# Two transformer blocks on one core: gate tiles in the scan's last quarter, attention turns further behind their scaling, inverse roots by logarithm and exponential

## What is computed

```python
# block 1: hx = modulate(rms_norm(x), ...), hc the same for 256 context tokens
o = hgrn_scan(forward) + flip(hgrn_scan(backward))     # 4 heads x 128, gated linear recurrence
att = softmax(q @ k.T / 8) @ v                         # 8 heads x 64, 2 kv heads, 768 keys
a = (rms_norm(o, per head) * silu(g_hg)) @ w_branch_a
b = att @ w_branch_b
x = x + g1 * ((sigmoid(ga) * a + sigmoid(gb) * b) @ w_out)
x = x + g2 * expert_choice_moe(modulate(rms_norm(x), ...))   # 16 experts, 64 tokens each
# block 2: norm, one projection, three-way sparse attention beside a short convolution,
# then x + rms_norm(...) @ w_o and x + square(relu(h @ w_up)) @ w_down
# rms_norm(x) = x * lax.rsqrt(mean(x * x) + 1e-6) * g
```

## Time and profile before

| | before |
|---|---|
| median of 3 runs | 2027.04 us (2026.67 to 2030.47) |
| profiled execution | 2034.27 us, span 2032.9 us |
| PE matmuls busy | 1773.4 us, 87% of the span |
| PE weight loads busy | 1145.5 us, 56% |
| DVE busy | 833.3 us, 41% |
| ACT busy | 540.9 us, 27% |
| POOL busy | 121.7 us, 6% |
| DMA | 329.38 MB, mean 162 GB/s |

### The profile page before, as it was taken

One profiled execution on the slowest core, in us unless ns is written; L12 is line 12 of the kernel. 1 busy time (PEld: TensorE's weight loads), 2 busy tenths in 40 slices (PEclk: granted clock), 3 DMA queues, 4 the chain that ended last, 5 costly groups with the idle time before them and its releaser, 6 DMA issues.

```text
span 2032.9 us, 20232 instructions
## 1 busy us (share of the span) xinstructions
PE 1773.4 (87%) x8121; PEld 1145.5 (56%) x8121; DVE 833.3 (41%) x1331; ACT 540.9 (27%) x963; POOL 121.7 (6%) x127
## 2 busy tenths in 40 slices
PE   5999799967899884888888888899888899999998
PEld 2657567645677662233233333387645478888876
DVE  2164744664533334011110111437566644444443
ACT  2234543643322322000000000223354432222221
POOL 0002111111000001000000000000100101001110
PEclk9999899978999896999999999999997699999999
DMA  8121201222404322999999999532400022322201
GB/s 316 65 66 45 80 21 63 83 83 84 124 1 172 124 83 79 423 421 422 421 421 422 421 421 421 202 123 91 128 31 0 1 83 94 114 83 83 96 29 42
DMA packets 92449, 329.38 MB, mean 162 GB/s; under 512 B 7493, under 2 KB 22725, under 8 KB 67781
## 3 DMA queue, kind: packets, MB, share of 16 engines
q1 hardware_dynamic: 85408, 315.80, 40.2%
q10 hardware_dynamic: 5604, 8.04, 1.2%
q0 software_dynamic: 1344, 4.25, 0.6%
HBM read 322.82 MB, written 4.19 MB: 161 GB/s over the span
## 4 chain that ended last, share of the span: by engine, by line
PE 66%; DMA 14%; DVE 11%; ACT 4%; issue 3%; SPq 1%; ACTq 0%; DVEq 0%
PE PS L633 21%; PE PS L734 8%; PE PS L965 8%; DMA ring<-in_w_exp_down_dram 6%; PE PS L374 6%; DMA ring<-in_w_exp_gate_dram 5%; PE PS L370 3%; PE PS L505 3%; PE PS L745 2%; PE PS L589 2%; PE PS L800 2%; PE PS L430 1%; DVE wR L1613 1%; DMA ring<-in_w_mod_dram 1%; PE PS L473 1%
## 5 line engine op out<-in xcount | busy, mean ns | idle before, releaser
L633 PE MATMUL PS<-hR,wR 128*128 128x512 f32 x1200 | 300.0, 409 | 27.2 <-DVE wR L1613 13.2
L633 PEld LDWEIGHTS PS<-hR,wR 128*128 128x128 f32 x1200 | 231.8, 195 | 92.2 <-issue 27.1
L734 PE MATMUL PS<-ring,xeT 128*64 128x512 f32 x1024 | 231.1, 602 | 39.1 <-DMA ring<-in_w_exp_gate_dram 36.7
L1613 DVE TENSOR_TENSOR wR<-ring,wR 128x1024 fp32r<-128x1024 f32 (+2 forms) x142 | 161.1, 1135 | 249.5 <-ACT wR L1068 249.3
L1068 ACT CAST wR<-ring 128x1024 fp32r<-128x1024 f32 (+2 forms) x142 | 138.3, 975 | 213.7 <-PE PS L965 126.4
L734 PEld LDWEIGHTS PS<-ring,xeT 128*64 128x64 f32 x1024 | 77.2, 138 | 191.7 <-issue 185.3
L965 PE MATMUL PS<-wR,hR 128*128 128x512 f32 x768 | 176.1, 390 | 8.9 <-DVE tmp L2341 6.9
L633 PE MATMUL PS<-xR,wR 128*128 128x512 f32 x768 | 175.3, 389 | 0.0
L965 PEld LDWEIGHTS PS<-wR,hR 128*128 128x128 f32 x768 | 143.5, 188 | 41.4 <-DVE tmp L2341 9.6
L633 PEld LDWEIGHTS PS<-xR,wR 128*128 128x128 f32 x768 | 144.1, 188 | 29.8
L734 PE MATMUL PS<-ring,hidT 128*64 128x512 f32 x512 | 115.2, 596 | 25.4 <-DMA ring<-in_w_exp_down_dram 19.6
(11 more groups left out here) (400 smaller groups left out, 2229.4 us busy)
## 6 DMA issues: line engine op xcount, KB each, us to landing
ring<-in_w_exp_gate_dram SPq DMA_DIRECT2D x64, 1024.0 KB, 13.7
ring<-in_w_exp_up_dram SPq DMA_DIRECT2D x64, 1024.0 KB, 13.7
ring<-in_w_exp_down_dram SPq DMA_DIRECT2D x64, 1024.0 KB, 12.8
ring<-in_w_mod_dram SPq DMA_DIRECT2D x12, 2048.0 KB, 8.2
ring<-in_w_in_dram SPq DMA_DIRECT2D x11, 2048.0 KB, 13.1
ring<-in_w_up_dram SPq DMA_DIRECT2D x8, 2048.0 KB, 9.2
ring<-in_w_down_dram SPq DMA_DIRECT2D x8, 2048.0 KB, 7.9
ring<-in_w_in_dram SPq DMA_DIRECT2D x9, 1024.0 KB, 5.3
```

The costliest lines, as they stand in the source:

```text
L633: mm = T.matmul(b, o[s][:, k, :], x[t][:, k, :], start=(k == ks[0] and j == 0), stop=(k == ks[-1] and j == 2))
L734: mm = T.matmul(b[es, ns], stat[:, 2 * kq + k, es], W.view(units[e2])[:, k, ns], start=(kq + k == 0), stop=(kq == 3 and k == 1))
L1613: V.tensor_tensor(lo, W.view(unit)[:, ks, cs], hi.bitcast(F32), ALU.subtract) \
```

## The change

Seven things change together.

1. **Gate tiles.** The four gate tiles leave `mix` and run as filler of the fourth quarter (`gate_tiles`), two steps of six matmuls per round. Their weights have a chunk buffer of their own, `wRg`; five of the activations' eight high parts are cast in the third quarter (`tokens_ahead`), and their low part lies in two pieces (`hR1l`, `hR1m`), because parts of the memory are in use until late; `GATE_K` orders the pieces accordingly. ACT and DVE get `gate_weights` as filler.
2. **Attention.** It now ends within the first three quarters: `FILL` becomes `((1,), (1, 1, 2), (1, 2))`, a cycle of counts. In `attention_order` a step's turns stand one score pair later, and ahead of the step's own scaling, and the values of a step come in the step but one behind it.
3. **Modulations.** `MODS` gives each quarter a wait and a list: 5 and 6, then 7 (after 12 rounds), then 8, 9 and 10, then 11. Weight 7 is loaded before the last gate's weights `("b", 1)`.
4. **Order of the branches and of the ring.** The first four `mg` tiles of the first branch run in a row, then four pairs of `wb` and `mg`, then the four `wb` tiles left. Their gates lie in four places of `uT`. The weight units follow the order in which they are used. Chunks 4 to 7 use `wRg` too.
5. **Head sums** of the second pair of heads stand behind the first `mg` tile and not ahead of the gate tiles.
6. **Inverse roots** (first and second pair of heads, ahead of the router, after the experts, in `select`, in `ffn`) are `exp(-0.5 * ln(scale * sum + eps))`, two ACT instructions (`inverse_root`); scaling and `reciprocal` on DVE go.
7. **Masks and gains** are issued behind the rope table in `qkv` and not in `setup`.

```diff
-FILL = (1, 1, 1, 2)
-MODS = ((5, 6), (), (7, 8), (9, 10, 11))
+FILL = ((1,), (1, 1, 2), (1, 2))
+MODS = ((6, (5, 6)), (12, (7,)), (6, (8, 9, 10)), (0, (11,)))
+GATE_K = (0, 1, 2, 6, 7, 3, 4, 5)
...
-    for x in (("f", 0), 4, ("q", 0), ("v", 0), ("b", 0), 5, 6, ("f", 1), ("q", 1), ("v", 1), ("b", 1), 7, 8, 9, 10, 11):
+    for x in (("f", 0), 4, ("q", 0), ("v", 0), ("b", 0), 5, 6, ("f", 1), ("q", 1), ("v", 1), 7, ("b", 1), 8, 9, 10, 11):
...
-    for br, (a, wb, rows_of) in enumerate(((3328, "w_branch_a", cols), (4352, "w_branch_b", head_cols))):
-        u += [(("wb", br), *rows_of(d[wb], 0, 1024)), (("mg", br, 0), *cols(d["w_in"], a, 512)),
-              (("mg", br, 1), *cols(d["w_in"], a + 512, 512))]
+    u += [(("mg", 0, 0), *cols(d["w_in"], 3328, 512)), (("wb", 0), *cols(d["w_branch_a"], 0, 1024)),
+          (("mg", 0, 1), *cols(d["w_in"], 3840, 512)), (("wb", 1), *head_cols(d["w_branch_b"], 0, 1024)),
+          (("mg", 1, 0), *cols(d["w_in"], 4352, 512)), (("mg", 1, 1), *cols(d["w_in"], 4864, 512))]
...
-    left = list(programs)
+    left, counts = list(programs), itertools.cycle(n)
     while left:
         left = [g for g in left if next(g, "end") != "end"]
-        for _ in range(n):
+        for _ in range(next(counts)):
...
-    hR1 = [m4.take(f"hR1{i}", [128, 8, 512], F32R) for i in range(2)]
+    hR1h, hR1l = m4.take("hR1h", [128, 8, 512], F32R), m4.take("hR1l", [128, 6, 512], F32R)
+    sq1 = m4.take("sq1", [128, 2, 512])
     wR1 = m4.take("wR1", [128, 2, 2, 1024], F32R)
     aR, tm = (m4.take("aR", [128, 4, 512], F32R), aRl), m4.take("tm", [128, 512])
-    sq1 = Area(nc, KEEP + 8192, HT).take("sq1", [128, 2, 512])
+    m4 = Area(nc, KEEP + 4096, HT)
+    wRg, hR1m = m4.take("wRg", [128, 2, 2, 1024], F32R), m4.take("hR1m", [128, 2, 512], F32R)
...
+    mix_chunks += mg[0][:4]
+    for t in range(8):
+        mix_chunks += wb[0][t:t + 1] + mg[0][t + 4:t + 5]
+    for t in range(8):
+        mix_chunks += mg[1][t:t + 1] + wb[1][t:t + 1]
...
-        def modulation(pool, js):
-            if not js:
-                return
-            for n in range(6 if js[-1] < 9 else 0):
+        def modulation(pool, wait, js):
+            for n in range(wait):
...
+        def gate_tiles(pool):
+
+            for n in range(6):
+                yield
+            for n, (key, *_) in enumerate(mix_chunks[:4]):
+                b = pool.take(T, key, dve_mix["silu", n])
+                T.wait_ge(*dve_lo[key])
+                o = parts(wRg, mix_chunks, n)
+                for i, k in enumerate(GATE_K):
+                    if n == 0:
+                        T.wait_ge(*dve_mix["hR", k])
+                    for j, (s, t) in enumerate(TERMS):
+                        mm = T.matmul(b, o[s][:, k, :], hR1(t, k), start=(i + j == 0), stop=(i == 7 and j == 2))
+                    if i == 7:
+                        mm.then_inc(pe_mm.sem, pe_mm.up((key, 0)))
+                    if i % 2:
+                        yield
 
         def mix():
             pool = Banks(0, 6)
-            total = Banks(6, 7).take(T, "total1", dve_mix["total"])
...
+                    if n == 4:
+                        for h in range(2, 4):
+                            b = pool.take(T, ("hn", h), act_mix["hn", h])
+                            T.wait_ge(*act_mix["sq", h])
+                            T.matmul(b, ones, sq1[:, h - 2, :], start=True, stop=True) \
+                                .then_inc(pe_mix.sem, pe_mix.up(("hn", h)))
...
-            weave([combine(levels, q)] + ([prepare(gates, q + 1)] if q < 3 else []) + [modulation(gates, MODS[q])] +
+        for q in range(3):
+            weave([combine(levels, q), prepare(gates, q + 1), modulation(gates, *MODS[q])] +
                   ([head_norms()] if q == 2 else []), both, FILL[q])
         for _ in both:
+            pass
+        ahead = gate_tiles(rest)
+        weave([combine(levels, 3), modulation(gates, *MODS[3])], ahead, (2,))
+        for _ in ahead:
             pass
         W.free["scan"] = pe_scan["o", 3, 2]
...
-        for n in range(17):
-            for x in range(2):
-                if n < 16:
-                    scores(2 * n + x)
-                if n:
-                    turn_p(n - 1, x)
-                yield
+        for n in range(18):
+            if n < 16:
+                scores(2 * n)
+            if n % 2 and n > 1:
+                values(n - 2)
+            yield
+            if n < 16:
+                scores(2 * n + 1)
+            if 1 <= n < 17:
+                turn_p(n - 1, 0)
+            yield
+            if 1 <= n < 17:
+                turn_p(n - 1, 1)
             if n < 16:
                 scale(n)
-            if n and n % 2 == 0:
-                values(n - 1)
             yield
 
...
+        def inverse_root(to, src, scale, s, key, bias=None):
+
+            A.activation(to, src, ACT.Ln, bias=eps if bias is None else bias, scale=scale).then_inc(s.sem, s.up())
+            A.wait_ge(*s.last)
+            A.activation(to, to, ACT.Exp, scale=-0.5).then_inc(s.sem, s.up(key))
...
-            for i, (name, o) in enumerate((("q_norm_g", 0), ("k_norm_g", 0), ("g_q_2", 0), ("g_k_2", 0), ("g_k_2", 64),
-                                           ("g_k_2", 128), ("b_cmp2_2", 0), ("b_cmp2_2", 64))):
-                A.dma_start(gb[:, i, :], d[name][o:o + 64].partition_broadcast(128)).then_inc(s_gb, 16)
-            A.dma_start(mstage, d["k_masks"]).then_inc(s_masks, 16)
...
+            copy_hi(wRg, mix_chunks, 5)
+            gate(0)
+            gate(1)
+            gated(0)
+            gate(2)
+            gated(1)
+            gate(3)
+            copy_hi(wRg, mix_chunks, 6)
+            for h in range(2, 4):
+                A.wait_ge(*pe_mix["hn", h])
+                inverse_root(sq1[:, h - 2, :], bank(("hn", h))[:, 0:512], 1.0 / 128, s, ("hn", h))
+            copy_hi(wRg, mix_chunks, 7)
+            branch_gate(0, 0)
+            branch_gate(0, 1)
+            gated(2)
+            copy_hi(wR1, mix_chunks, 8)
+            branch_gate(0, 2)
+            gated(3)
+            copy_hi(wR1, mix_chunks, 9)
+            branch_gate(0, 3)
+            for n in range(10, len(mix_chunks) + 1):
...
-            A.activation(rinv, rinv, ACT.Sqrt).then_inc(s.sem, s.up("rinv"))
+                after(mix_chunks[n - 1][0])
+            A.wait_ge(*pe_mix["sqy", 7])
+            inverse_root(rinv, bank("total1")[:, 0:512], 1.0 / 1024, s, "rinv")
...
-                    A.wait_ge(*dve_sec["cN2"])
-                    A.activation(rinv, rinv, ACT.Sqrt).then_inc(s.sem, s.up("rinv"))
-                    A.activation(cN, cN, ACT.Sqrt).then_inc(s.sem, s.up("cN"))
+                    A.wait_ge(*dve_sec["rm"])
+                    A.activation(rinv, bank(("total2", 0))[:, 0:512], ACT.Ln, bias=eps, scale=1.0 / 1024) \
+                        .then_inc(s.sem, s.up("lnr"))
+                    A.wait_ge(*dve_sec["total"])
+                    A.activation(cN, cN, ACT.Ln).then_inc(s.sem, s.up())
+                    A.wait_ge(*s.last)
+                    A.activation(cN, cN, ACT.Exp, scale=-0.5).then_inc(s.sem, s.up("cN"))
+                    A.activation(rinv, rinv, ACT.Exp, scale=-0.5).then_inc(s.sem, s.up("rinv"))
...
+        def tokens_ahead():
+            for n in range(8):
+                yield
+            A.wait_ge(*pe_scan["o", 1, 2])
+            A.wait_ge(*dve_scan["y", 1, 6])
+            for k in range(5):
+                tokens((k,))
+                yield
+
+        def gate_weights():
+            A.wait_ge(*dve_scan["y", 2, 6])
+            tokens((5, 6, 7))
+            yield
+            A.wait_ge(*pe_att.end)
+            copy_hi(wRg, mix_chunks, 0)
+            yield
+            copy_hi(wRg, mix_chunks, 1)
+            yield
+            yield
+            yield
+            copy_hi(wRg, mix_chunks, 2)
+            yield
+            yield
+            copy_hi(wRg, mix_chunks, 3)
+            yield
 
...
-                    s.also("cN2")
-                    V.wait_ge(*act_sec["cN"])
-                    V.reciprocal(cN, cN).then_inc(s.sem, s.up())
-                    V.reciprocal(rinv, rinv).then_inc(s.sem, s.up("rinv"))
+                    V.wait_ge(*act_sec["rinv"])
```

More of the change, by code:

```diff
@@ L1 @@
+import itertools
 from contextlib import ExitStack
@@ L768, in experts @@
             pool = Banks(6, 8)
-            total = [pool.take(T, ("total2", i), dve_sec["total"]) for i in range(2)]
+            total = [pool.take(T, ("total2", i), (act_sec["lnr"], dve_sec["total"])[i]) for i in range(2)]
             T.wait_ge(*pool_moe["gmat"])
@@ L1163, in mod_rows, with modulation @@
             A.copy(mrow, bank(("mod", j))).then_inc(act_mod.sem, act_mod.up(("row", j)))
-        def modulation(js):
-            if not js:
-                return
-            for n in range(6 if js[-1] < 9 else 0):
+        def modulation(wait, js):
+            for n in range(wait):
                 yield
@@ L2400, in dve @@
         both = attention()
```

(5 more changed lines are left out.)

266 lines of the change are left out of this document (128 added, 138 removed).

## The result

The changed kernel takes 1997.0 us in the median (1996.2 to 2000.3, 4 runs), the kernel before 2028.8 (2026.7 to 2031.4, 4 runs): ratio 0.9846 with a 95% interval of 0.9828 to 0.9864, some 32 us less. Forecast was 1990. The profiled executions are 37 us apart (2034.3 and 1997.1): the profiled one of before lies 6 us above its median.

The account below looks back on a forecast made before the run. TensorE bounds the kernel with 66% of the path, its scan quarters losing time to waits when thinly filled. Terms -30 + 5 - 4.5 - 2.8 - 2.2 - 2.7 = -37 from 2027.0 give 1990 us, range 1967 to 2010.

Parts of the forecast that it names:

- Scan and gates, -30: From the scan's first diagonal product to the first branch tile: 354 us instead of 383.5, content plus chosen losses by quarter.
- the third quarter's loss: Scan's third quarter: 18 us lost beyond its content, before 20; two reciprocals leave DVE, the last attention steps run bare.
- lower bound: Scan and gate tiles: losses as low as 1 us a quarter would give -64 instead of -30.
- Density is what changes: Scan quarters: reason for choosing -30 between -64 and -10, nearer to the dense second quarter than to the last.
- rival (a): Scan: density cures all, two-step distance removes 18 us of late turns; 22 us less, 1968; chance 0.20.
- Rival (d), the clock,: End of third quarter and last quarter run at 1.2 GHz; up to 2041, slower by 14; chance 0.04.
- Rival (b): Last quarter: gates not hidden, weights late or POOL, ACT, DVE chain sets the pace; 18 more, 2008; chance 0.13.
- Rival (c), losses in proportion,: First three quarters: work waits on ACT, losses 15, 17, 22; +19, 2009; chance 0.10.
- Start of the branches and ring order, +5 and -4.5: Branches: head sums +2 and stall 3 at the start; second branch's weight wait and slow first tile go, -4.5.
- Masks, -2.8: Kernel start: masks and gains no longer share the engines with the fourth modulation weight; -2.8 us (0 to -3.3).
- Inverse roots, -2.2 and -2.7: Ahead of the router -2.2 us, after the experts -2.7, by logarithm and exponential on ACT.
- A later site costed at nothing: Two later inverse roots hide behind products: 0; if they did not, 2 us each.

## Why the prediction was right

The sign, the size (32 of 37 us) and the range held, but the largest term is made up otherwise than forecast. It fell 7 us short, and the smaller terms together gave 4.0 more than they were priced at, so the sum came out better than its parts: that is luck.

- **Scan and gates, -30:** the profiles show -23.0. By quarter forecast and found are 76 and 76.4, 122 and 125.5, 97 and 105.8, 59 and 52.7. The last quarter lost 1.7 us against its content, not 8, and is shorter than the 55 to 62 that the forecast gave as its sign. The step that failed is the third quarter's loss, 18 us in the forecast and 27 in the trace: its clock stayed at 0.85, and from the outputs at 443 us to the next quarter's start at 467 PE is busy for 13.8 of 23.7 us at 0.78, with two turns 3.0 and 5.1 us late. The forecast said "run bare" and priced it 9 us too low (6 to 7 in the profiles where this quarter takes 103.3). Its lower bound also has a slip: with 1 us lost in each quarter, contents of 64, 117, 79 and 51 give 315 us and so -68, not -64.
- **"Density is what changes":** half wrong. The gate tiles' density in the last quarter is worth 25 us (undone), but the attention's order, which the forecast did not price by itself, is worth 33 us undone and 18 alone in the kernel before. The account by stretch: gates and last quarter gain 57.8 us (110.5 to 52.7), and the first three quarters, with the attention squeezed in, grow by 34.7 with the new order (273.1 to 307.8) and by 61.9 with the old (335.0). Set beside the kernel before with the new order (268.6), the squeeze costs 39. With the old order it costs all that the gates gain, and that kernel stands where the kernel before does.
- **The waits that go:** rival (a) had the two-step distance remove the 18 us of late turns. They stayed (19.1 us); the scores' 13.7 us went, and the two runs on the order show that the order takes them away. That a score pair no longer stands behind a late turn is the likely reason, read from the order and not tested by itself.
- **Rival (d), the clock,** came in the end of the third quarter, where six turns took 1.5 us, and not in the last one: 0.64 is what that gets without filling; with it 0.97. Rival (b) did not come: in the last quarter no gate tile waits for its weights.
- **Rival (c), losses in proportion,** came in part. The first three quarters lost 12.4, 8.5 and 26.8 us, 47.7 in all, where the forecast had 35 and this rival 54; the third lost more than the rival's 22. The last quarter's 6 us to the good hid half of that.
- **Start of the branches and ring order, +5 and -4.5:** from the end of the gate tiles to the last output sum it is 206.5 us before and 204.4 after, -2.1 for a forecast of +0.5. PE's waits for weights there sum to 4.9 us before (3.00 of it in the earlier trace rows) and 3.0 after (2.07 of it new, at 540 us); the rest is the wait of 0.19 ahead of a tile, which stood in 10 places and stands in 5. The ring alone gave 3.8. The two terms were sized well: the head sums took 1.9 us, and the wait of 2.07 is followed by eight matmuls at 0.63 us and not 0.39, another 1.9. What makes the stretch shorter all the same is the fewer small waits (1.0), four slow matmuls fewer at the output projection (1.0) and 1.5 us that are not placed.
- **Masks, -2.8:** between the profiles 4.0 (163.0 to 158.9), undone 2.4 to 3.8.
- **Inverse roots, -2.2 and -2.7:** between the profiles -3.0 and -2.8, undone 2.4 and 4.5. The second was sized too low: the root is worth 3.8 to 4.0, and the expert products ahead of it took 1.0 us longer in the changed kernel (480.0 and 479.0). A later site costed at nothing is not quite free: in `ffn` two loads make PE's last turns 0.37 us late, and the stretch ahead of it is 0.7 us longer (75.0 to 75.7).

The terms found add up to -23.0 - 2.1 - 4.0 - 3.0 - 2.8 + 0.7 = -34.2; with the two stages told above (-4.9, which the changed kernel did not repeat, and +2.1, of which 1.6 are the slow matmuls) it is the 37.0 between the two spans. The medians give 31.8.

## What to carry to other kernels

Look for the stretch in which a busy engine pauses briefly between dependent steps, and read its clock: filling it with work that is due anyway is worth the idle time and the clock together, here 22.8 us of gate tiles for nothing. In a hand-written order, put a consumer behind one more unit of independent work than its producer needs; a late consumer holds up everything behind it, so judge such a move by all waits of the engine and not by its own row. And profile several kernels that share a stage before reading a difference of 5 us in it: two profiles of one kernel agreed to 0.1 us in quarters that differ by up to 4.7 among kernels with the same order there.

## What was not expected of the hardware

With bare levels in the last quarter, 16 matmuls, a state product and 1.3 us of wait in every 5.9 us, the granted clock stayed at 0.50 for 24 us, and a level took 3.68 us and not 1.90; with twelve matmuls of a gate tile between two levels it took 1.89. The same program gives 121.2 or 126.1 us for one stage from one execution to the next, at clocks of 0.88 and 0.83; all fourteen profiles lie at one of these or between. Logarithm and exponential, each time in a row, took a table load of 1.28 us each.
